# Gate tables of half of the dense tokens by accumulating indirect DMAs instead of one-hot products on TensorE

## The reference

```python
h = h + concat([ya, yb]) @ w_out                 # the mixer's output, residual
xf = rmsnorm(h, norm_ffn_g)                      # (1024, 1024)
q = (xf @ w_query).reshape(T, 8, 2, 128)         # 8 heads, two half queries
s = einsum('thpc,hpkc->thpk', q, sub_keys)       # 128 scores for each half
s1, i1 = top_k(s[:, :, 0], 16); s2, i2 = top_k(s[:, :, 1], 16)
# best 16 of the 256 sums s1 + s2; expert = i1 * 128 + i2
gates = softmax(top_s)                           # 16 per head, 128 per token
act = gelu(einsum('tkd,td->tk', expert_u[idx], xf))
h = h + einsum('tk,tkd->td', gates * act, expert_v[idx])
out = rmsnorm(h, norm_final_g)
```

## Time and profile before

| | us |
|---|---|
| median of three timed runs | 2735.07 (2734.32 to 2739.5) |
| the profiled execution | 2742.4 |
| its span in the trace | 2740.7 |
| TensorE busy | 2562.8 (94%) |
| VectorE busy | 2070.5 (76%) |
| GpSimd busy | 1264.7 (46%) |
| ScalarE busy | 386.7 (14%) |
| DMA | 857.88 MB, mean 313 GB/s |

### The profile page before, as it was taken

One profiled execution on the slowest core, in us unless ns is written; L12 is line 12 of the kernel. 1 busy time (PEld: TensorE's weight loads), 2 busy tenths in 40 slices (PEclk: granted clock), 3 DMA queues, 4 the chain that ended last, 5 costly groups with the idle time before them and its releaser, 6 DMA issues.

```text
span 2740.7 us, 25175 instructions
## 1 busy us (share of the span) xinstructions
PE 2562.8 (94%) x8172; PEld 1473.0 (54%) x8172; DVE 2070.5 (76%) x4369; ACT 386.7 (14%) x731; POOL 1264.7 (46%) x1038
## 2 busy tenths in 40 slices
PE   7999999989676799999999999999999999999992
PEld 6888888878666444444444444444444444444441
DVE  2307978779799677777778778678787686877989
ACT  1111111111788300000010010000001000000010
POOL 0000110101233255645666657566566676756765
PEclk9999999999999999999999999999999999999996
DMA  5343655534788989888899999999999999999998
GB/s 206 138 172 144 250 205 186 205 123 149 238 243 249 336 290 339 277 338 288 294 385 378 420 388 364 416 369 410 404 398 412 381 378 414 393 416 399 404 398 323
DMA packets 279763, 857.88 MB, mean 313 GB/s; under 512 B 23504, under 2 KB 95184, under 8 KB 265040
## 3 DMA queue, kind: packets, MB, share of 16 engines
q0 software_dynamic: 148608, 541.13, 51.8%
q1 hardware_dynamic: 124912, 298.36, 29.5%
q10 hardware_dynamic: 6112, 16.78, 1.6%
HBM read 807.94 MB, written 48.23 MB: 312 GB/s over the span
## 4 chain that ended last, share of the span: by engine, by line
PE 53%; DMA 14%; DVE 11%; POOL 11%; issue 9%; ACT 1%; another core or an unknown queue 1%; ACTq 0%; DVEq 0%; POOLq 0%
PE pairs L624 16%; PE pairs L506 16%; PE pairs L612 14%; POOL ring L489 11%; DMA ring<-in_expert_v,idx 7%; DMA ring<-in_expert_u,idx 6%; DVE arena L1082 5%; PE pairs L549 4%; DVE arena L906 2%; DVE junk L895 1%; DVE arena L1078 1%; PE pairs L579 1%; DVE xf L906 1%; DMA arena<-in_uT 1%; PE pairs L516 1%
## 5 line engine op out<-in xcount | busy, mean ns | idle before, releaser
L489 POOL DMA_INDIRECT ring<-in_expert_u,idx x512 | 695.3, 1358 | 1021.8 <-DVE dots L895 748.6
L612 PE MATMUL pairs<-arena 128*128 128x512 f32 x2048 | 886.4, 594 | 12.0 <-DMA arena<-in_uT 6.9
L624 PE MATMUL pairs<-arena 128*128 128x512 f32 x2048 | 882.2, 592 | 5.2 <-DVE arena L953 5.2
L489 POOL DMA_INDIRECT ring<-in_expert_v,idx x512 | 563.9, 1101 | 295.1 <-DVE arena L906 129.1
L895 DVE CUSTOM_DVE_ANT_0 junk<-ring,xf 128x1024 bf16<-128x1024 f32 x512 | 609.5, 1222 | 114.0 <-DMA ring<-in_expert_u,idx 107.8
L612 PEld LDWEIGHTS pairs<-arena 128*128 128x128 f32 x2048 | 390.0, 191 | 505.3 <-issue 497.6
L624 PEld LDWEIGHTS pairs<-arena 128*128 128x128 f32 x2048 | 388.9, 190 | 496.0 <-issue 495.7
L906 DVE SCALAR_TENSOR_TENSOR arena<-ring,arena 128x1024 f32<-128x1024 f32 x381 | 472.2, 1282 | 91.7 <-DMA ring<-in_expert_v,idx 88.6
L506 PE MATMUL pairs<-arena 128*128 128x272 f32 (+1 forms) x2048 | 464.0, 389 | 13.5 <-DVE arena L977 7.3
L506 PEld LDWEIGHTS pairs<-arena 128*128 128x128 f32 x2048 | 391.7, 192 | 82.1 <-DVE arena L977 7.8
L748 ACT ACTIVATE arena<-pairs 128x512 f32<-128x512 f32 x128 | 75.4, 596 | 1524.7 <-PE pairs L612 1228.4
(11 more groups left out here) (124 smaller groups left out, 956.9 us busy)
## 6 DMA issues: line engine op xcount, KB each, us to landing
arena<-in_w_all SPq DMA_DIRECT2D x80, 1024.0 KB, 4.9
arena<-in_uT SPq DMA_DIRECT2D x128, 512.0 KB
arena<-in_expert_v SPq DMA_DIRECT2D x128, 512.0 KB
gate_tables<-arena SPq DMA_DIRECT2D x16, 2048.0 KB
arena<-gate_tables SPq DMA_DIRECT2D x32, 1024.0 KB
ring<-in_expert_u,idx POOLq DMA_INDIRECT x512
ring<-in_expert_v,idx POOLq DMA_INDIRECT x512
arena<-in_hT SPq DMA_DIRECT2D x4, 1088.0 KB, 8.0
```

The costliest lines, as they stand in the source:

```text
L489: nc.gpsimd.indirect_dma_start(out=ring[:, r % RING, :], out_offset=None, in_=expert_u if table == "u" else expert_v, in_offset=bass.Indir ...
L612: last = nc.tensor.matmul(s_bank[x % 4], uslot[:, x % USLOTS, k * P:(k + 1) * P], xfT[:, k, :], start=(k == 0), stop=(k == KD - 1))
L624: last = nc.tensor.matmul(o_bank[n % 4], gated[:, x % GSLOTS, t * P:(t + 1) * P], vrows[:, j, half * 512:(half + 1) * 512], start=(j == 0) ...
```

## The change

The groups now go dense, gathered, dense, gathered (`BASE`). The first group's two tiles are dense but get their part of the tables in another way. Four stores on ScalarE's queue write zeros to the tables' share of these 256 tokens (4 x 4.2 MB from a cleared `junk`). When a tile is ranked, VectorE also computes, for each of its 128 choices per token, the place of that (i, j, token) in the flat table (`place`), and the gates are normalised at once (`spread`). GpSimd then scatters them: one indirect DMA per choice k, 128 tokens x one float, with an addition in the memory (`compute_op=ALU.add`). Within a head no place repeats; between heads it may, so before each head's 16 DMAs it waits until all earlier ones of the tile have landed. The table stage keeps only the other two dense tiles: 32 batches and 8 chunks. Gathered rows may now be taken only from the last group on (`take(us, n == GRPS - 1)`) and in the table stage.

```diff
-BASE = (512, 0, 256, 768)
+BASE = (0, 512, 256, 768)
-DENSE_GROUP = {1: 0, 2: 1}
-GATHERED_RANK = {0: 0, 1: 1, 6: 2, 7: 3}
-DENSE_RANK = {2: 0, 3: 1, 4: 2, 5: 3}
+DENSE_GROUP = {0: 0, 2: 1}
+SCATTER_RANK = {0: 0, 1: 1}
+GATHERED_RANK = {2: 0, 3: 1, 6: 2, 7: 3}
+DENSE_RANK = {4: 0, 5: 1}
-BATCHES = DT // HOTS
+BATCHES = TABLED * P // HOTS
+ZEROED = 4
...
-        COST = {"keys": 6.8, "cands": 1.4, "pairs": 6.2, "digits": 3.4, "pick": 3.9, "keep": 0.7, "row": 1.35}
+        COST = {"keys": 6.8, "cands": 1.4, "pairs": 6.2, "digits": 3.4, "pick": 3.9, "keep": 2.0, "spread": 1.5, "row": 1.35}
...
-                elif rows < 2 * HK and (0 if rows < HK else 1) in ranked:
+                elif with_rows and rows < 2 * HK:
...
+                    two = two[:2] + [("spread", a, 0)] + two[2:] + [("next place", 0, 0), ("spread", b, 0)]
...
             sp.wait_ge(table_full, 2 * BATCHES)
             for j in range(VJ):
                 load_v(0, j)
...
+            for t in range(SCATTERED):
+                sp.wait_ge(scattered[t], 16 * HK)
             load_gates(0)
...
+            nc.gpsimd.memset(zeros, 0.0).then_inc(zero_ready, 1)
+            pool.wait_ge(zeroed, 16 * ZEROED)
+            for t in range(SCATTERED):
+                pool.wait_ge(s_gates, t + 1)
+                for h in range(HEADS):
+                    if h > 0:
+                        pool.wait_ge(scattered[t], 16 * TOPK * h)
+                    for k in range(h * TOPK, (h + 1) * TOPK):
+                        nc.gpsimd.indirect_dma_start(out=g_flat, out_offset=bass.IndirectOffsetOnAxis(ap=place[:, t, k:k + 1], axis=0),
+                                                     in_=gate[:, t, k:k + 1], in_offset=None, compute_op=ALU.add).then_inc(scattered[t], 16)
...
-            for t in range(DENSE_TILES):
+            for t in range(TABLED):
                 for m in range(3):
                     last = nc.tensor.transpose(bank[4 + t][:, m * P:(m + 1) * P], route[:, m, t, :], ident[:])
...
+            def spread_after(kind, n, i):
+                for t in exp_after[kind, n, i]:
+                    act.wait_ge(s_shifted, t + 1)
+                    nc.scalar.activation(gate[:, t, :], gate[:, t, :], ACT.Exp).then_inc(s_exped, 1)
...
+                if kind == "bcv" and n == 0 and i < ZEROED:
+                    g = HALF_GROUPS // ZEROED
+                    act.wait_ge(zero_ready, 1)
+                    act.dma_start(g_d[i * g:(i + 1) * g, :, 0:FIRST_CHUNK, :].rearrange("g p c n -> p g (c n)"),
+                                  zeros.unsqueeze(1).to_broadcast([P, g, FIRST_CHUNK * GJ * CHUNK])).then_inc(zeroed, 16)
...
+                if r in SCATTER_RANK:
+                    t = SCATTER_RANK[r]
+                    a, b = scratch[:, 0:HK], scratch[:, HK:2 * HK]
+                    ju, jh = (scratch[:, n * HK:(n + 1) * HK].bitcast(U32) for n in (2, 3))
+                    nc.vector.tensor_tensor(gate[:, t, :].rearrange("p (h k) -> p h k", h=HEADS), best[:], low, ALU.subtract).then_inc(s_shifted, 1)
+                    nc.vector.tensor_copy(ju, half_i[:, 1, :])
...
+                    nc.vector.scalar_tensor_tensor(out=place[:, t, :], in0=jh, scalar=float(P * CHUNKS * GJ * CHUNK - GJ * CHUNK), in1=b,
+                                                   op0=ALU.mult, op1=ALU.add)
...
+                elif kind == "spread":
+                    dve.wait_ge(s_exped, a + 1)
+                    normalise(gate[:, a, :].rearrange("p (h k) -> p h k", h=HEADS), HEADS).then_inc(s_gates, 1)
```

More of the change, by code:

```diff
@@ L237, in program @@
         out_kept = sem("out_kept")
+        s_shifted = sem("s_shifted")
+        s_exped = sem("s_exped")
+        s_gates = sem("s_gates")
+        zero_ready = sem("zero_ready")
+        zeroed = sem("zeroed")
+        scattered = [sem(f"scattered{t}") for t in range(SCATTERED)]
         d_shifted = sem("d_shifted")
@@ L280, in ranking_of, with take @@
                     + [("digits", r, 0)] + [("pick", r, q) for q in range(4)] + [("keep", r, 0)])
[L282 removed]
+        plan, to_rank = {}, []
         rows = 0
[L285 removed]
+        def take(us, with_rows):
             nonlocal rows
[L287 to L288 removed]
+            got, spent = [], 0.0
+            while spent < us:
                 if to_rank:
                     unit = to_rank.pop(0)
[L291 to L293 removed]
+                    if unit[0] == "next place":
+                        break
+                elif with_rows and rows < 2 * HK:
                     unit = ("row", rows, 0)
@@ L298, in take @@
                 got.append(unit)
-                us -= COST[unit[0]]
-            return got
+                spent += COST[unit[0]]
+                if unit[0] == "keep":
+                    kept_at[unit[1]] = spent
+            return got
+        kept_at, exp_after = {}, {s: [] for s in steps}
+        QUERY_US = 14.2
         for n in range(GRPS):
             if n > 0:
-                to_rank += ranking_of(GT * (n - 1)) + ranking_of(GT * (n - 1) + 1)
-            for place, us in FILL:
-                plan[n, place] = take(us)
+                one, two = ranking_of(GT * (n - 1)), ranking_of(GT * (n - 1) + 1)
+                if GT * (n - 1) in SCATTER_RANK:
+                    a, b = SCATTER_RANK[GT * (n - 1)], SCATTER_RANK[GT * (n - 1) + 1]
+                    two = two[:2] + [("spread", a, 0)] + two[2:] + [("next place", 0, 0), ("spread", b, 0)]
+                to_rank += one + two
+            for where, us in FILL:
+                plan[n, where] = take(us, n == GRPS - 1)
+                for kind, r, _ in plan[n, where]:
+                    if kind == "keep" and r in SCATTER_RANK:
+                        if where == "query":
+                            late_by = int((kept_at[r] + 2.0) / QUERY_US)
+                            after = ("query", n, late_by) if late_by < 4 else ("score", n, min(3, 2 * (late_by - 4) + 1))
+                        else:
+                            after = {"conv0": ("bcv", n, 1), "conv1": ("bcv", n, 2), "conv2": ("bcv", n, 3), "conv3": ("bcv", n, 4),
+                                     "gate": ("bcv", n, 5), "y": ("bcv", n, 5), "outp": ("ynorm", n, 0)}[where]
+                        exp_after[after].append(SCATTER_RANK[r])
         assert not to_rank
         for b in range(BATCHES):
-            plan["hots", b] = take(HOT_FILL) if b % 2 else []
+            plan["hots", b] = take(HOT_FILL, True) if b % 2 else []
         first = [("row", r, 0) for r in range(rows, 2 * HK)]
@@ L1040, in _ @@
             norm_x(0)
+            dve.wait_ge(const_pool, 3)
+            nc.vector.tensor_scalar(token_u[:, 1:2], token_u[:, 0:1], 5, None, ALU.logical_shift_right)
+            dve.drain()
+            nc.vector.scalar_tensor_tensor(out=token[:, 0:1], in0=token_u[:, 1:2], scalar=float((GJ - 1) * CHUNK), in1=token_u[:, 0:1],
+                                           op0=ALU.mult, op1=ALU.add)
+            dve.drain()
+            for t in range(1, SCATTERED):
+                nc.vector.tensor_scalar(token[:, t:t + 1], token[:, 0:1], float(t * P * GJ), None, ALU.add)
             for n in range(GRPS):
```

52 lines of the change are left out of this document (34 added, 18 removed).

## The result

The changed kernel takes 2833.73 us (median; 2827.21 to 2835.83), the kernel before 2736.05 us (2734.32 to 2739.5) on the same chip: ratio 1.0351, 95% interval 1.0331 to 1.0371. It is slower by 3.5%; I had forecast 2670 and a chance of 0.75 that it is faster.

What follows compares the result with a forecast made beforehand. Bounds: TensorE in projections, VectorE in the table stage, TensorE and DMA engines in the dense pass. 2742.4 - 103.6 + 37 + 0 + 1 = 2676.8, less 7.3 for the timed median: 2669.5, rounded to 2670 us; range 2630 to 2775.

Steps and rivals of the forecast that it cites:

- What bounds the kernel: Projections at TensorE's pace, table stage at VectorE's, the long dense stretch by TensorE and DMA engines (share 1.00, 396 GB/s).
- Part 1: Table stage: 32 batches in place of 64, 16 pairs of steps at 6.38 us fall away, gain 103.6 us.
- Part 2: Dense pass: 40 more gathered rows, 12 hidden by TensorE's matmuls, 28 paid by their bytes at 396 GB/s, +37 us.
- Part 3: GpSimd's queue ahead of the first gathered row: 256 accumulating DMAs take 369 us, end at 681, cost nothing.
- slack: Before VectorE misses its first gathered row: a row by 697 us costs nothing; forecast at 688, 9 us earlier.
- The packets that I costed at nothing: Projections: each scatter DMA gives 8 tiny packets to each of 16 engines, 0.8 us per DMA at most, costed at nothing.
- Rival 1: GpSimd's queue: the scatter is slow enough to eat the gain; at 1.84 us spacing 129 us late, 2799 us; chance 0.22.
- Part 4: Start of the projections: four zero stores of 4.2 MB, down by 128 us, cost nothing or a few us, taken as 1.
- Rival 3: Projections: clearing or tiny packets hold them up, the first x tile 80 us late, 2750 us; chance 0.08.
- Rival 2: Dense pass: it swallows the 28 rows at no cost, giving 2633 us; chance 0.17.
- the v rows: Gathers beside two-input L906: mean issue 1.10 us, median 0.937, so a two-input operation was taken hardly to matter.

Runs made afterwards that it cites:

- no scatter: The changed kernel without the scatter's DMAs and SyncE's wait for them, clearing, tables and row order kept: 2683.57 us, ratio 0.9784.
- six heads: The changed kernel with six of eight rounds of accumulating DMAs per scattered tile, 192 in place of 256: 2702.09 us, ratio 0.9863.
- plain: The changed kernel with its 256 scatter DMAs overwriting instead of adding: 2982.57 us, ratio 1.0868.
- by turns: The changed kernel with the two scattered tiles' rounds alternating, so one is issued while the other's lands: 2806.06 us, ratio 1.0213.
- The run of the forms: No kernel: groups of 16 indirect DMAs of each kind alone, then adding ones beside three VectorE instructions; adding 4-byte issue 1560 ns.

## Why the prediction was wrong

**What bounds the kernel** held: projections at TensorE's pace, the table stage at VectorE's, the dense pass with the DMA engines full (1.00, 397 GB/s after, 396 before).

**Part 1, the table stage**: -103.6 forecast, -103.4 measured; the 16 pairs of batches stand in the chain from 862.54 us on, 15 of them by the rows of L1180, (951.93 - 862.54) / 14 = 6.39 us each.

**Part 2, the rows that move**: +37 forecast, +32.3 measured between the two traces, which is too low by up to the 13 us that they lack of the medians' difference. Four other runs move the same 40 rows, on other chips, and their dense pass takes 1872.6 us (no scatter), 1875.7 (six heads), 1878.3 (plain) and 1882.1 (by turns), so +43.5 to +53.0. Taken by the medians instead, as the whole difference less that of the two earlier stages, the changed kernel gives +45, and the ratios of no scatter, by turns and six heads 45 to 49. So 37 was a little small. As forecast TensorE's new waits are for VectorE's gate multiplications, 32.9 us against 5.2. So the mechanism held, and the size within some 10 us.

**Part 3, the scatter on GpSimd's queue: here it failed**, in one term, the price of an issue. Start (312 against 310.9), count, 14 waits, landings (36.4 against 37.2 us in all) and slack (697) were right; that the landings fit is luck, for their 2.6 us came from an ordinary store of 512 KB. The issue was priced from the gathers, 1.00 us and a gap of 0.30, because "no accumulating DMA is in the trace" and the value would be "much nearer the lower, by the kind of work beside it". It is 1.582 and 0.36: 256 x 0.582 = 149 us and 16 us of gaps. With the landings' 1 us that makes 535 in place of 369, last one out at 846, first row at 852.6 in place of 688; less the 9 us of slack, that is the 155.9 us by which the table stage starts late. The runs that show it: without the addition the issue falls to 0.971 us; by itself it is 1.56 against 0.97 us; a quarter fewer DMAs give back 135 of 139 us by this price.

My working asked what the work on VectorE does to the issue, and took the wrong axis. The same 1.55 us stands in the run by itself, where VectorE is idle, and in the 150 us of the changed kernel in which no other engine works. The extra belongs to the operation. The bounds of 331 to 694 us held the 535, and the upper one stood for a cost of 316 us, which the range of the forecast, ending at 2775, never took in. I took the value by the neighbour that was alike in descriptors and let the difference in kind, the addition, weigh nothing in it. The packets that I costed at nothing cost the projections nothing: the page's queue q0 carries 36864 more of them, nine for each DMA engine and DMA where I had eight, and TensorE kept its pace.

**Rival 1** is what happened. Its spacing of 1.84 us ("one more overhead for the accumulation") is 0.1 us under the 1.945 measured (535 less 37.2 us of landings, over 256 DMAs), which is 27 of the 35 us between its 2799 and 2834; its deciding point of 1.59 us was passed by far. I gave it 0.22, though no row showed such an issue and with 256 of them each 0.1 us was 26 us.

**Part 4, clearing**: nothing. L1116 wants its first x tile at 125.89 us against 126.88, and without the scatter the first batch begins 2 us earlier than before. **Rival 3** (projections held up) is out by the same rows and by TensorE's 367.95 us in their window. **Rival 2** (the dense pass swallows the rows) is out by part 2's 32 us and more.

**What stands beside the issue.** The run of the forms shows 1576 and 1572 ns beside TENSOR_SCALAR and MAX8 with short operands, and 2172 beside TENSOR_TENSOR with two inputs. My reading of the v rows, that "a two-input operation as such hardly matters", does not hold for this form. The Trainium skill, page "SBUF — State Buffer", section Who interferes with whom, says that a VectorE instruction with two SBUF inputs contends with a GpSimd instruction that reads SBUF, and infers further on that tensor_tensor still leaves the making of descriptors alone. The run of the forms agrees with the first, which I had not weighed, and not with the second; that the adding DMA reads SBUF at that moment is not shown. In the kernel it matters little, since the mean beside ranking is 1.58 us and beside the batches 1.68.

## What to carry to other kernels

An operation that the trace doesn't hold has to be priced by what is different in it, not by what is alike: where the count is in the hundreds and the queue serial, one small run of that instruction alone (16 of them sufficed here) decides more than all the rest of the working. A long serial job on one queue must stand behind, or between, what others wait for soon; the kernel was 98 us slower with these 256 DMAs ahead of the first row, and 42 us faster when no early row stood behind them. A long wait that is named after a short transfer sends the reader to the queue it was issued from. And two traces are two executions: where the medians differ by more than the spans do, a piece read off the spans is off by as much.

## What the runs showed of the hardware

- An indirect DMA of 128 elements costs GpSimd 0.95 to 0.97 us as a gather or a plain scatter, and 1.56 us as an adding scatter, for 4 bytes and 4 KB alike; the gap to the next is 0.30 us.
- Adding 4 bytes keeps the DMA engines busier than overwriting does: share 0.23 against 0.02 in the windows above, at a lower pace of DMAs (48 in 90 us against 45 in 60).
- Beside a VectorE TENSOR_TENSOR of 128x1024 with two inputs an adding issue takes 2.17 us in place of 1.56 (means of 16).
- Beside four-byte indirect DMAs without addition TensorE fell, in one run, to a thirteenth of its matmuls (18 in place of 234 in 50 us), with a granted clock of 0.50 once it had idled; the same program ran without it on another chip. Cause open.
